# Low parts of fourteen weight units of the mixer's input projection: from VectorE to GpSimd

## What is computed

```python
def _mixer(h_ctx, h_lat, rows, w_in, conv_w, ...):
    p_ctx = h_ctx @ w_in
    p_lat = h_lat @ w_in
    p_ctx = concatenate([_conv_seq(p_ctx[..., :CONV_CH], conv_w[1]), p_ctx[..., CONV_CH:]], -1)
    p_lat = concatenate([_conv_grid(p_lat[..., :CONV_CH], conv_w, rows), p_lat[..., CONV_CH:]], -1)
    u = concatenate([p_ctx, p_lat], axis=1)
    mq, mk, rr, rk, rv, mv, mo, gates, lw_f, lw_b, la, lg = split(u, SPLIT_POINTS, axis=-1)
```

## Time and profile before

| | us |
|---|---|
| median of three runs | 3040.67 |
| profiled execution | 3040.06 |
| its span, first to last instruction | 3038.2 |
| busy in the span: PE | 2844.0 (94%) |
| DVE | 1838.6 (61%) |
| ACT | 1269.9 (42%) |
| POOL | 789.7 (26%) |

### The profile page before, as it was taken

One profiled execution on the slowest core, in us unless ns is written; L12 is line 12 of the kernel. 1 busy time (PEld: TensorE's weight loads), 2 busy tenths in 40 slices (PEclk: granted clock), 3 DMA queues, 4 the chain that ended last, 5 costly groups with the idle time before them and its releaser, 6 DMA issues. The chain is left out here.

```text
span 3038.2 us, 54412 instructions
## 1 busy us (share of the span) xinstructions
PE 2844.0 (94%) x22525; PEld 2300.6 (76%) x22525; DVE 1838.6 (61%) x2584; ACT 1269.9 (42%) x1628; POOL 789.7 (26%) x427
## 2 busy tenths in 40 slices
PE   9889999999999999999999989878989799999994
PEld 7467888889777777888868877567885488888883
DVE  3657663210333444666246977676756699889997
ACT  3544232222333334332234321423332277777775
POOL 2013444434332312444420000010000134444531
PEclk9999999999999999999999999889999799999997
DMA  4643522232221212222222200241003499999996
GB/s 172 225 151 111 97 97 97 97 134 92 84 70 57 70 57 97 86 96 96 96 98 111 70 23 12 84 158 46 32 18 123 160 346 363 356 366 364 372 363 260
DMA packets 83394, 440.91 MB, mean 145 GB/s; under 512 B 19712, under 2 KB 22784, under 8 KB 34816
## 3 DMA queue, kind: packets, MB, share of 16 engines
q1 hardware_dynamic: 73920, 429.63, 38.9%
q0 software_dynamic: 9280, 8.43, 0.8%
HBM read 423.30 MB, written 37.77 MB: 152 GB/s over the span
## 5 line engine op out<-in xcount | busy, mean ns | idle before, releaser
L85 POOL TENSOR_TENSOR ring_lo<-ring,unit_hi 128x2048 fp32r<-128x2048 f32 x110 | 507.1, 4610 | 1039.4 <-ACT unit_hi L74 1039.4
L146 PE MATMUL wide<-h_hi,unit_hi 128*128 128x512 f32 x1296 | 517.0, 399 | 16.1 <-POOL ring_lo L85 6.3
L148 PE MATMUL wide<-h_hi,ring_lo 128*128 128x512 f32 x1296 | 507.5, 392 | 0.0
L147 PE MATMUL wide<-h_lo,unit_hi 128*128 128x512 f32 x1296 | 506.6, 391 | 0.0
L3480 DVE TENSOR_TENSOR ex_w_lo<-ring,ex_w_hi 128x2048 fp32r<-128x2048 f32 x194 | 441.9, 2288 | 44.2 <-ACT ex_w_hi L3475 43.0
L3475 ACT CAST ex_w_hi<-ring 128x2048 fp32r<-128x2048 f32 x194 | 369.2, 1908 | 110.9 <-DMA ring<-in_weights 96.2
L74 ACT CAST unit_hi<-ring 128x2048 fp32r<-128x2048 f32 x114 | 217.5, 1908 | 370.5 <-PE wide L148 366.2
L146 PEld LDWEIGHTS wide<-h_hi,unit_hi 128*128 128x128 f32 x1296 | 244.5, 189 | 76.3 <-issue 10.8
L148 PEld LDWEIGHTS wide<-h_hi,ring_lo 128*128 128x128 f32 x1296 | 244.2, 188 | 52.3
L147 PEld LDWEIGHTS wide<-h_lo,unit_hi 128*128 128x128 f32 x1296 | 244.9, 189 | 49.4 <-issue 0.7
L432 DVE TENSOR_TENSOR ffn_hidden_lo<-ffn_whole,ffn_hidden_hi 128x512 f32 (+1 forms) x44 | 201.2, 4573 | 53.0 <-ACT ffn_hidden_hi L403 53.0
(11 more groups left out here) (573 smaller groups left out, 5609.7 us busy)
## 6 DMA issues: line engine op xcount, KB each, us to landing
ring<-in_weights SPq DMA_DIRECT2D x356, 1024.0 KB, 5.8
rw_F<-factors SPq DMA_DIRECT2D x9, 1024.0 KB, 5.1
factors<-rp_out SPq DMA_DIRECT2D x4, 1280.0 KB, 5.3
factors<-rp_out SPq DMA_DIRECT2D x4, 1024.0 KB, 5.3
ex_both<-pair_rows_out SPq DMA_DIRECT2D x4, 1024.0 KB, 7.9
x<-in_x SPq DMA_DIRECT2D x8, 256.0 KB, 6.8
x_kept<-x SPq DMA_DIRECT2D x1, 2048.0 KB, 12.8
x<-x_kept SPq DMA_DIRECT2D x1, 2048.0 KB, 7.9
```

The lines of the kernel that those rows point to most:

```text
L85: pool.tensor_tensor(self.lo[n % RING][:, :], self.ring[n % RING][:, :], self.hi[n % 2][:, :].bitcast(F32), ALU.subtract).then_inc(self.lo ...
L146: pe.matmul(dst, a[0], b[0], start=start, stop=False)
L147: pe.matmul(dst, a[0], b[1], start=False, stop=False)
L148: return pe.matmul(dst, a[1], b[0], start=False, stop=stop)
```

## The change

The low parts of units 2 to 15 are taken out of DVE's order and put into POOL's, between the clearing of the gates' buffers and the wait for all units. The low parts of units 0 and 1 stay with DVE (in `Entry.vector`).

```diff
@@ block.gpsimd
             pool.wait_ge(entry.stored, 16)
             gates.gpsimd(pool)
+            pool.wait_ge(gates.cleared, 6)
+            pool.wait_ge(w.lo_ready, w.split_at(w.at + 2))
+            for n in range(2, U_IN):
+                w.write_lo(pool, 0, n)
 
             pool.wait_ge(w.used, w.at + U_IN)
@@ block.vector
             entry.vector(dve, w)
-            following = 2
             for n, (kind, m) in enumerate(items):
                 if kind != "conv":
                     continue
                 grid, seq = pads[m % 2]
-                while following <= min((n + 1) // 2 + 1, U_IN_COLUMNS):
-                    w.write_lo(dve, 0, following)
-                    following += 1
                 dve.wait_ge(copied, n + 1)
@@
-            w.write_lo(dve, 0, U_IN - 1)
             dve.wait_ge(w.used, w.at + U_IN)
```

## The result

The changed kernel takes 3066.94 us (median of six runs, 3061.2 to 3069.95) against 3038.25 us before (six runs, 3029.55 to 3044.88). The ratio, estimated from the runs themselves and not from the two medians, is 1.0086, with a 95% interval from 1.0068 to 1.0105: slower by 0.9%, close to the forecast (3070, +1.0%). The two profiled executions have spans of 3062.5 and 3038.2 us, a difference of 24.3.

A forecast was written before the change was run, and what follows sets the result against it. DVE was taken to set the pace of the stage's second half. Later dense stretch +20.7, blocks +27.0, writes gone -13.2, conv 17 no longer ahead -6.7, ACT's copies +1.9: +29.7 on 3040.06, so 3070 us, range 3048 to 3086.

The forecast's parts named there:

- Unit 2: POOL's first low part waits for the store of x, so PE begins unit 2 at 1628.3, 17.3 us late.
- Low clock after it: PE's first 12 matmuls after the hole run at the lower clock, costing 2.4 us; a longer rest adds 2 to 5.
- Early units: PE goes on alone through units 3 to 6, each POOL low part in time; it ends unit 6 at 1694.5.
- Start of the dense stretch: DVE's conv 6, after which DVE does not rest, ends at 1707.8, 20.7 us later than before.
- Blocks: Six POOL writes (units 9 to 14) each hold up a DVE tap 4.5 us, from a 5.13 us row: +27.0.
- Unit 14: PE begins unit 14 at 1816.3, 29.7 us later than before, after a hole of some 16 us ended by ACT's copy.
- Behind it: Units 14 and 15 follow as before (35.2 us), unit 15's low part hidden by PE's 17 us at unit 14.
- The whole: Whole kernel: 3040.06 + 29.7 = 3070 us, given 0.67.
- A: Rival: POOL does not hold up DVE's taps, so only +3, 3043 us; chance 0.12.
- C: Rival: faster, DVE freed of its writes closes both PE holes, -15, 3025 us; chance 0.02.
- D: Rival: POOL's block costs a tap about half, 2.3 us in place of 4.5, so 3055 us; chance 0.13.
- B: Rival: DVE holds POOL off until DVE waits for another engine; 6 to 8 us more, 3077 us; chance 0.06.

The follow-up runs named there:

- only_unit2: The kernel before with unit 2's low part alone written by POOL, behind the store of x; 3061.09 us, 1.0075 of before, stage +17.6 us.
- store_later: The changed kernel with POOL writing units 2 and 3 before its wait for the store of x; 3048.85 us, 1.0029 of before, stage +8.1 us.
- memset: The changed kernel with POOL's fourteen subtractions replaced by memsets of the same tile, which read nothing from SBUF; 3038.33 us, 1.0006 of before.
- one_read: The changed kernel with POOL's fourteen subtractions replaced by multiplications by zero that read one SBUF tensor; 3062.25 us, 1.0074 of before.

## Why the prediction was right

Times of after are moved by the 2.88 us of the earlier entry, to stand beside the prediction's.

- **Unit 2.** Forecast: PE begins unit 2 at 1628.3, 17.3 us late. Measured: 1628.29, with a hole of 17.04. The agreement to 0.01 us is in part luck, since POOL's write began 0.2 us earlier than forecast and took as much longer (1623.39 to 1628.24). That only this wait stands in its way, `only_unit2` and `store_later` showed from both sides.
- **Low clock after it.** Forecast 2.4 us by the hole of 6.14 us, and perhaps 2 to 5 more for the longer rest. Measured less: from 1625.41 to 1628.84 eight matmuls in 3.43 us in place of 1.84, so 1.6. After the hole of 15.62 us it was 2.6: from 1811.03 to 1816.59, 13 matmuls in 5.56 us in place of 3.0. A longer rest did not cost more here, so the 2 to 5 us more that the range allowed for it were not needed.
- **Early units.** PE was not stopped again until unit 13, as forecast; the writes of units 4 to 8 made long taps that nobody waited for long.
- **Start of the dense stretch.** Forecast: conv 6 ends at 1707.8, 20.7 us later. Measured: 1707.2, 20.1 later.
- **Blocks.** Forecast 4.5 us each, between 0 and 5.3. Measured: the six long taps of units 9 to 14 add up to 29.85, less six times 0.75 is 25.35, or 4.2 each. The row of 5.13 us was the right one to go by, and the 4.4 that it gives is nearer than the 4.5 that was taken.
- **Unit 14.** 20.1 + 25.4 - 13.2 - 6.7 + 1.9 = 27.5, against a forecast of 29.7. Measured: 1811.03 + 2.88 is 27.3 later than 1786.62. What ended the hole was ACT's copy, as forecast, and the hole was 15.62 us where "some 16" was named.
- **Behind it.** Unit 15's low part was in time; PE had no further hole.
- **The whole.** 3066.94 against 3070. The stage became 27.5 us longer, 2.2 under the forecast, mostly because of the blocks (25.4 against 27.0). The medians differ by 28.7, and the spans of the two profiled executions by 24.3. That the whole comes out as near as 3 us is therefore in part luck, with parts outside the stage that differ by up to 10 us between profiles; the stage's own terms are what bears the forecast out.

The rivals: A fell with the 14 long taps, and `memset` shows that its time (+3 forecast, +1.7 measured) was right for taps that are free. C fell with the store. D fell with blocks of 4.2. Of B a part is true. The prediction said that POOL gets in after at most one tap, and for four of the six writes of units 9 to 14 that holds (4.7 to 5.2 us). But the writes of units 9 and 12 took 6.07 and 6.26: at 1755.30 POOL asked while DVE was in the first instructions of a full convolution, and the one in flight and two more ran before POOL did, until about 1756.95 (the write's end less 4.6). These instructions follow each other without a pause, since the taps of the two sums do not wait for one another there. In five of the six cases the tap that was then blocked is one that DVE began 0.04 us after the end of the one before, in the short pause in which a tap waits for the last one's result. So POOL did mostly get in at a pause of DVE, as B has it, but a pause between two taps is enough, and it needs no wait for another engine. The write of unit 13 (1780.11, 4.67 us) and the row at 537.35 went ahead although DVE's instructions show no pause there, so by what rule the two take turns stays open. The delay was some 1.5 us twice on POOL, and nothing was seen to wait for it.

## What to carry to other kernels

Before moving elementwise work from VectorE to GpSimd, ask what VectorE will run at that time: if that reads two tensors from SBUF, as the taps here do, a GpSimd instruction that reads SBUF takes most of its time from VectorE too (4.2 of 4.6 us for the subtraction, 3.25 of 5.37 for the multiplication). A write of 4.6 us on GpSimd in place of one of 2.2 on VectorE then makes VectorE slower, not free. Look up in the trace what the new engine's queue has in front of the moved work; here a wait for a DMA, harmless until then, cost 17.6 us by itself. And where an engine is saturated and another waits for it, first see which of its work the other needs: moving 13 us of gate steps behind the last convolution made the stage some 15 us shorter with no work moved to another engine.

## What the runs showed of the hardware beyond that

- A memset of GpSimd over the same tile (1.81 us for 128 x 2048) ran beside 0.75-us taps with no sign of a collision, and a multiplication that reads a single tensor (`one_read`) did collide, so among these it took a read of SBUF by GpSimd.
- With one tensor read, GpSimd's instruction took 5.37 us and VectorE was shut out for 3.25 of it; with two tensors it took 4.6 and VectorE was shut out until about its end (the tap at 1720.67 ended 0.56 us after the write). The Trainium skill (SBUF — State Buffer, section "SBUF: two separate sides") has the port pair held for the whole instruction; the subtraction agrees (a block up to its end), the one-read instruction, by its recorded end, does not.
- GpSimd's multiplication of one tensor by a constant was slower than its subtraction of two of the same size (5.37 against 4.6 us).
- The loss at the lower clock level after a hole did not grow with the hole: 1.6 us after 17.04, 2.6 after 15.62, and 2.4 after 6.14. It also differs between executions: after the like hole of 17.93 us in `one_read` twelve matmuls took 0.63 us or more, after the 17.04 us here seven.
